# A gated feed-forward on TensorE: high weights against [high | low] in one 512-column matmul, in two of four layers

## The reference, cut to what matters

```python
def swiglu(h, w1, w3, w2):
    return (jax.nn.silu(h @ w1) * (h @ w3)) @ w2

# layers 2 and 3, behind their mixers
    h = rms_norm_2(x, norm_ffn_g_2[layer])
    x = x + swiglu(h, ffn_w1[layer], ffn_w3[layer], ffn_w2[layer])
```

## Time and profile before

| | us |
|---|---|
| median of 3 runs | 1327.35 (1326.54 to 1328.16) |
| span of the profiled execution, from its first to its last instruction | 1324.4 |
| TensorE busy in that span | 1296.3 (98%) |
| GpSimd busy | 1006.1 (76%) |
| ScalarE busy | 682.9 (52%) |
| VectorE busy | 637.0 (48%) |

### The profile page before, as it was taken

One profiled execution on the slowest core, in us unless ns is written; L12 is line 12 of the kernel. 1 busy time (PEld: TensorE's weight loads), 2 busy tenths in 40 slices (PEclk: granted clock), 3 DMA queues, 4 the chain that ended last, 5 costly groups with the idle time before them and its releaser, 6 DMA issues.

```text
span 1324.4 us, 27666 instructions
## 1 busy us (share of the span) xinstructions
PE 1296.3 (98%) x10976; PEld 1247.4 (94%) x10976; DVE 637.0 (48%) x1163; ACT 682.9 (52%) x944; POOL 1006.1 (76%) x793
## 2 busy tenths in 40 slices
PE   6999999999999999999999999999999999999999
PEld 6889999999988889999999978999999999999998
DVE  8994465555555748455565574211113455311112
ACT  7725643444666756443457565434446566543342
POOL 1327888888777659888887794988887766988885
PEclk9999999999999999999999999999999999999999
DMA  6305675545535235555454532555554433555530
GB/s 269 129 33 181 169 250 191 185 172 181 191 134 185 101 126 183 178 188 188 172 178 160 193 128 96 192 192 179 174 185 167 160 126 120 187 178 187 190 127 32
DMA packets 33879, 217.07 MB, mean 164 GB/s; under 512 B 3683, under 2 KB 7428, under 8 KB 8196
## 3 DMA queue, kind: packets, MB, share of 16 engines
q1 hardware_dynamic: 30096, 211.14, 45.1%
q10 hardware_dynamic: 3700, 4.75, 1.4%
HBM read 213.26 MB, written 2.62 MB: 163 GB/s over the span
## 4 chain that ended last, share of the span: by engine, by line
PE 85%; DVE 6%; ACT 6%; issue 2%; POOL 1%; DMA 0%; DVEq 0%; SPq 0%; ACTq 0%; POOLq 0%
PE up L1568 19%; PE up L1569 18%; PE up L1570 18%; PE acc L1568 7%; PE acc L1570 6%; PE acc L1569 6%; DVE opnd L972 2%; PE side L1795 2%; PE up L1703 1%; PE acc L1761 1%; ACT w_hi L503 1%; ACT opnd L641 1%; PE side L1576 1%; PE up L1834 1%; PE acc L1933 0%
## 5 line engine op out<-in xcount | busy, mean ns | idle before, releaser
L413 POOL TENSOR_TENSOR w_lo<-ring,w_hi 128x512 fp32r<-128x512 f32 x748 | 955.4, 1311 | 235.7 <-ACT w_hi L503 231.8
L1568 PE MATMUL up<-opnd,w_hi 128*128 128x256 f32 x2064 | 592.3, 287 | 3.7 <-DVE opnd L972 1.5
L1569 PE MATMUL up<-opnd,w_lo 128*128 128x256 f32 x2064 | 583.9, 283 | 0.0
L1570 PE MATMUL up<-opnd,w_hi 128*128 128x256 f32 x2064 | 583.8, 283 | 0.0
L503 ACT ACTIVATE w_hi<-ring 128x2048 fp32r<-128x2048 f32 x188 | 358.9, 1910 | 264.4 <-PE up L1570 202.7
L1568 PEld LDWEIGHTS up<-opnd,w_hi 128*128 128x128 f32 x2064 | 395.6, 192 | 16.1 <-issue 13.1
L1569 PEld LDWEIGHTS up<-opnd,w_lo 128*128 128x128 f32 x2064 | 395.8, 192 | 1.3 <-issue 1.0
L1570 PEld LDWEIGHTS up<-opnd,w_hi 128*128 128x128 f32 x2064 | 395.7, 192 | 0.0
L1568 PE MATMUL acc<-opnd,w_hi 128*128 128x256 f32 x784 | 223.0, 284 | 1.2 <-DVE x L1218 1.2
L1569 PE MATMUL acc<-opnd,w_lo 128*128 128x256 f32 x784 | 221.8, 283 | 0.0
L1570 PE MATMUL acc<-opnd,w_hi 128*128 128x256 f32 x784 | 221.8, 283 | 0.0
(11 more groups left out here) (296 smaller groups left out, 1421.3 us busy)
## 6 DMA issues: line engine op xcount, KB each, us to landing
ring<-in_stream SPq DMA_DIRECT2D x197, 1024.0 KB, 4.9
bias_rows<-mix ACTq DMA_DIRECT2D x1, 1536.0 KB
mix<-in_s_b SPq DMA_DIRECT2D x1, 1024.0 KB, 5.6
x<-in_x SPq DMA_DIRECT2D x1, 1024.0 KB, 7.7
mix<-in_s_c SPq DMA_DIRECT2D x1, 1024.0 KB, 11.7
mix<-bias_rows ACTq DMA_DIRECT2D x1, 1024.0 KB, 5.4
out_x<-x SPq DMA_DIRECT2D x8, 128.0 KB, 1.7
mix<-in_p ACTq DMA_DIRECT2D x2, 256.0 KB, 3.4
```

The source lines that it names most:

```text
L413: ins = nc.gpsimd.tensor_tensor(w_l[:, cols], ring[:, r, cols], w_h[:, cols].bitcast(f32), ALU.subtract)
L1568: MM(o, l_hi, r_hi, start=start, stop=False, skip_group_check=True)
L1569: MM(o, l_lo, r_hi, start=False, stop=False, skip_group_check=True)
L1570: return MM(o, l_hi, r_lo, start=False, stop=stop, skip_group_check=True)
```

## The change

In ffn2 and ffn3 alone (`WIDE`), the two products with the high weights become one matmul: the moving operand is [high | low], 512 columns, and writes 512 columns, high*high in the first half of a bank and high*low in the second. The product with the low weights stays at 256 columns and is added to the first half. A slot then has 32 matmuls, and its two halves take a bank each. Slots alternate between the two `up` banks and the two `side` banks. For this the operand is laid out as [partition, k, part, token], for all stages.

Behind the slot the halves are summed: ScalarE copies both second halves (the rest) to SBUF, VectorE adds them to the first halves, and multiplies by rstd in place, in PSUM. Silu reads there; the hidden product goes where the rest of the value was. So the banks of a tile are told free (`up_free`) at the end of the tile. ScalarE makes the copy ahead of the high part of slot k + 3. The first wide slot waits until every slot before it is told free. In the second slot PE makes the gate's half first, with `all_sums` behind its first group, and waits for rstd before it writes the value's half, since that bank held the sums.

```diff
+WIDE = (2, 3)
...
-        opnd = [sb("opnd0", [P, 2, KT, T], f32r)]
-        opnd.append(sb("opnd1", [P, 2, KT, T], f32r))
+        opnd = [sb("opnd0", [P, KT, 2, T], f32r)]
+        opnd.append(sb("opnd1", [P, KT, 2, T], f32r))
...
-        up = [ctx.enter_context(nc.psum_tensor(f"up{i}", [P, 2, T], f32)) for i in range(2)]
+        ups = ctx.enter_context(nc.psum_tensor("up", [P, 2, 2, T], f32))
+        up = [ups[:, i] for i in range(2)]
...
+        wide = [ups[:], side[:].rearrange("p m (a t) -> p m a t", a=2)]
...
                 def slot(k, i=None):
 
+                    j, part = (0, k) if k < 2 else ((k + 1) // 3, (k - 2) % 3)
+                    if l in WIDE and part != 2:
+                        act.wait_ge(sem("mm_done"), S + k + 1 if i is None else i * RING + (S + k + 1))
+                        c.up(A(f_c[:, 0:2], wide[part][:, :, 1], ACT.Copy), "rest_sb")
                     if i is None:
                         high_parts_to(S + k + 3)
...
+                    pair = wide[part]
+                    gate, val, h = (pair[:, 0, 0], pair[:, 1, 0], pair[:, 1, 1]) if l in WIDE else (gate_ps, val_ps, h_ps)
+                    if l in WIDE:
+                        c.wait("rest_sb")
+                        step(V.tensor_tensor(pair[:, :, 0], pair[:, :, 0], f_c[:, 0:2], ALU.add))
+                        r = rstd[:].unsqueeze(1).broadcast_to([P, 2, T])
...
+                            c.up_and_wait(V.tensor_tensor(pair[:, :, 0], pair[:, :, 0], r, ALU.mult), "g_ready")
...
-                    c.up_and_wait(V.tensor_tensor(hl, h_ps, hh.bitcast(f32), ALU.subtract), "h_ready")
+                    c.up_and_wait(V.tensor_tensor(hl, h, hh.bitcast(f32), ALU.subtract), "h_ready")
+                    if l in WIDE:
+                        c.tell("up_free")
...
+            def pair_products(o, l_hi, l_lo, r, start, stop):
+
+                MM(o, l_hi, r, start=start, stop=False, skip_group_check=True)
+                return MM(o[:, 0], l_lo, r[:, 0], start=False, stop=stop, skip_group_check=True)
...
+            def wide_slot(name, s, first, i=None, sums=False, fold=None, order=range(KT)):
+
+                slot_ready(s, i)
+                u = used[0]
+                used[0] += 1
+                pe.wait_ge(sem("up_free"), u if u == first else u - 1 if i is None else i * 4 + (u - 1))
+                o, w_h, w_l, both = wide[(u - first) % 2], weights_hi(s), weights_lo(s), opnd[SET[name]]
+
+                def part(k, m):
+                    w = slice((2 * k + m) * P, (2 * k + m + 1) * P)
+                    return pair_products(o[:, m], w_h[:, w], w_l[:, w], both[:, k], k == order[0], k == order[-1])
+
+                if sums:
+                    for j, k in enumerate(order):
+                        c.wait("hi_ready")
+                        c.wait("lo_ready")
+                        for m in range(2):
+                            ins = part(k, m)
+                        if j == KT // 2 - 1:
+                            square_sums(0)
+                else:
+                    for m in range(2):
+                        if fold is not None and m:
+                            pe.wait_ge(sem("rstd"), fold)
+                        for k in range(KT):
+                            ins = part(k, m)
+                            if fold is not None and m == 0 and k == 0:
+                                all_sums()
+                c.up(ins, "mm_done")
+                if sums:
+                    square_sums(1)
```

More of the change, by code:

```diff
@@ L659, in tile @@
                 def tile(parity, part):
+                    gate, h_out = (wide[part][:, 0, 0], wide[part][:, 1, 1]) if l in WIDE else (gate_ps, h_ps)
                     c.wait("g_ready")
-                    c.up(A(f_gg[:, 0], gate_ps, ACT.Gelu_apprx_tanh if l < 2 else ACT.Silu), "gated")
+                    c.up(A(f_gg[:, 0], gate, ACT.Gelu_apprx_tanh if l < 2 else ACT.Silu), "gated")
                     c.wait("h_raw")
-                    c.up(A(opnd[1][:, 0, 2 * parity + part], h_ps, ACT.Copy), "h_hi")
+                    c.up(A(opnd[1][:, 2 * parity + part, 0], h_out, ACT.Copy), "h_hi")
                 def slot(k, i=None):
+                    j, part = (0, k) if k < 2 else ((k + 1) // 3, (k - 2) % 3)
+                    if l in WIDE and part != 2:
+                        act.wait_ge(sem("mm_done"), S + k + 1 if i is None else i * RING + (S + k + 1))
+                        c.up(A(f_c[:, 0:2], wide[part][:, :, 1], ACT.Copy), "rest_sb")
                     if i is None:
@@ L697, in pe_operand @@
                 for k in range(2):
-                    c.up(A(opnd[1][:, 0, 6 + k], f_pe[:, k], ACT.Copy), "pe_hi")
+                    c.up(A(opnd[1][:, 6 + k, 0], f_pe[:, k], ACT.Copy), "pe_hi")
             def ple(l, end):
@@ L1176, in tile @@
                     dve.wait_ge(sem("mm_done"), s + k + 1 if i is None else i * 6 + (s + k + 1))
+                    pair = wide[part]
[4 more added lines that the diff above has]
+                        r = rstd[:].unsqueeze(1).broadcast_to([P, 2, T])
+                        if conv:
+                            step(V.tensor_tensor(f_u[:, 0:2, 2:258], pair[:, :, 0], r, ALU.mult))
+                        else:
+                            c.up_and_wait(V.tensor_tensor(pair[:, :, 0], pair[:, :, 0], r, ALU.mult), "g_ready")
+                    elif conv:
+                        over_rms(f_u[:, 0:2, 2:258], u)
+                    else:
+                        over_rms(side[:, :, 0:T], u)
+                        c.tell("g_ready")
                     if conv:
-                        over_rms(f_u[:, 0:2, 2:258], u)
-                        for t, o in ((0, gate_ps), (1, val_ps)):
+                        for t, o in ((0, gate), (1, val)):
                             base = COLS["conv"][0] + (l * 22 * 8)
@@ L1208, in ffn @@
                 with dve.Fori(0, 4) as i:
-                    c.enter(i, **(dict(dve_step=20, up_free=4, g_ready=4, gated=4, h_raw=4, h_hi=4, h_ready=4) if conv
-                                  else dict(up_free=4, g_ready=4, gated=4, h_raw=4, h_hi=4, h_ready=4)))
+                    steps = 4 * (5 * conv + (l in WIDE) * (1 + conv))
+                    c.enter(i, up_free=4, g_ready=4, gated=4, h_raw=4, h_hi=4, h_ready=4,
+                            **({"dve_step": steps} if steps else {}), **({"rest_sb": 4} if l in WIDE else {}))
                     for j in (3, 4):
@@ L1852, in ffn, with up_part @@
                 order = [m for g in groups for m in (2 * g, 2 * g + 1)]
[L1853 to L1857, removed]
+                first = BANK[f"ffn{l}"]
+                assert used[0] == first
+                def up_part(s, i=None):
+                    if l in WIDE:
+                        wide_slot(name, s, first, i)
+                    else:
+                        up_slot(name, s, i)
+                if l in WIDE:
+                    wide_slot(name, S, first, sums=True, order=order)
+                    wide_slot(name, S + 1, first, fold=(2, 5, 8, 10)[l])
+                else:
+                    up_slot(name, S, fresh=True, sums=True, order=order)
+                    up_slot(name, S + 1, fold=True)
+                up_part(S + 2)
+                up_part(S + 3)
                 def down(s, parity, first=False, i=None):
@@ L1863, in ffn @@
                 down(S + 4, 0, first=True)
-                up_slot(name, S + 5)
-                up_slot(name, S + 6)
+                up_part(S + 5)
+                up_part(S + 6)
                 down(S + 7, 1)
```

23 lines of the change are left out of this document (10 added, 13 removed).

## The result

The changed kernel takes 1332.59 us (median of 5 runs, 1332.29 to 1332.91), the kernel before 1327.1 on the same chip (5 runs, 1326.54 to 1328.16). The ratio is 1.0041, 95% interval [1.0029, 1.0054]: slower by 5.5 us, a small difference that the interval tells from none. The forecast was 1330.4, +3.1 us, with the range 1323 to 1336. The sign was right, the size not quite. Of all executions in this document one stands apart in time: in the experiment "First wait and third slot" one took 1781.3 us at a mean granted clock of 0.66; it counts in that kernel's median, which it moves by less than 0.1 us, and not in its ratio.

The account below looks back on a forecast made before the run. The prediction took TensorE, busy 98% of the span, to bound the kernel. Matmuls -5.3, first waits +5.1 and third slots +3.3 gave +3.1 us: 1330.4 us, range 1323 to 1336 (the forecast's own 1328 to 1333).

Parts of the forecast that it names:

- The matmuls: Up slots of ffn2 and ffn3: a group falls from 0.360 to 0.3525 us, 704 groups, 5.3 us saved.
- Rival A: Wide matmuls follow at 0.216 us, groups 0.336: 16.9 us saved, total -8.5 us, 1318.9; chance 0.14.
- B: Rival: a wide matmul costs exactly two narrow ones, 0.360 us a group, nothing saved: +8.4 us, 1335.8; chance 0.12.
- The first waits: First wide slot waits for up_free of all earlier slots: 3.7 us lost in ffn2, 1.4 in ffn3, together 5.1.
- so it ends at 826.8 instead of 823.1: 3.7 us lost: ffn2's first slot, begun at about 820.2, was to take 6.59 us, as undisturbed in ffn3.
- The third slots: Slot 2 waits for slot 0's late tile to free its banks: 1.7 us in ffn3, 3.3 in both feed-forwards.
- The loop: Added ScalarE and VectorE work lies beside PE: no PE idle in the loops, GpSimd's waits for w_hi still 0.7.
- From span to median: The runs' median lies 2.95 us above the profiled span, so a span of 1327.5 gives 1330.4.
- Rival C: The four waits cost about 1 us less each, +4.4 instead of +8.4: total -0.9 us, 1326.4; chance 0.10.

Follow-up runs that it names:

- First wait and third slot: Changed kernel with the first wide slot's up_free wait two counts lower and ScalarE taking the first tile ahead of slot 3's high weights: 1324.22 us, ratio 0.9979.
- first experiment: Changed kernel with the first wide slot of each wide feed-forward waiting for up_free two counts lower: 1325.55 us, ratio 0.9988 to the kernel before.
- second: Kernel before with only the stricter up_free wait at the first slot of ffn2 and ffn3 added: 1333.88 us, ratio 1.0052.
- third: Changed kernel with 22 small fp32 matmuls into a free bank ahead of ffn2's first wait: 1330.9 us, ratio 1.0030 to the kernel before.
- four-layer version: Changed kernel with loosened first wait, first tile early and slot 3's high weights on VectorE, widened in all four feed-forwards (ffn0 keeps the full wait): 1333.96 us, ratio 1.0056.
- kernel with 384 columns: Changed kernel with the wide matmul cut from 512 to 384 columns, part of a product left out: 1293.19 us, one run.

## Why the prediction was nearly right

- *The matmuls*: 0.3525 us a group was forecast, 0.3533 measured; 704 x 6.7 ns = 4.7 us against 5.3. Rival A (0.336) and B (0.360) are out: at 512 columns the distance is 236 ns, not 216, and the two ways of making the same sums differ by 6.7 ns a group. The formula behind the 216 is given in the Trainium skill ("TensorE: Matmul & The Clock Gate", section "Back-to-back issue gap") for an isolated matmul, which the prediction didn't say; for a stream of weight loads and matmuls the same section has about 131 ns at 512 columns. The 236 ns of this trace agree with neither. The short burst of the earlier trace rows was a good guide to both: 235 ns and 117.5 by it, 236 and 117 in the loop.
- *The first waits*: the start of both slots came out as worked out: 820.46 for about 820.2, and 1.43 us in ffn3 for 1.4. What failed is the step "so it ends at 826.8 instead of 823.1: 3.7 us lost". It took the slot to run at the upper clock behind a pause of five microseconds. The clock was at half for 6.83 us, and the slot took 2.7 us more than forecast. The two first waits together cost 7.8 us, not 5.1, which is outside this term's own bounds of 3 and 7: those allowed for half a microsecond to one only, and for no fall of the clock. That the total stayed in its range, and just inside the narrower 1328 to 1333, is to that extent luck: the range was wide enough to hold a cost that nobody had put into it. Taking the pause away restored the clock (first experiment), the pause alone brought the fall (second), and filling it with matmuls kept the clock but not the time of the wait (third).
- *The third slots*: 1.6 each for 1.7; the rest's copy took 0.58 for 0.62, VectorE's two operations were covered as said. The experiment in which ScalarE takes the tile first removed the wait.
- *The loop*: no wait of PE in it, as said. GpSimd waits for the high weights 19.5 us over 29 slots, 0.67 us each, as before:

```profile
POOL w_lo L418 <- ACT w_hi L508: 19.5, 29, 1.6
```

- *From span to median*: the 2.95 us between them are not all around the span. The execution after took 1332.91 us for a span of 1331.1, 1.8 around it; about half of the rest is that the execution of before was quick in its front (0.6 us quicker than the mean of the eleven other profiled executions). By the traces the forecast lacked 3.2 us (clock 2.7, groups 0.6, third slots -0.1), by the medians 1332.6 - 1330.4 = 2.2. The interval of the ratio is 3.8 to 7.2 us of difference and holds both 5.5 and the 6.3 of the account; the remaining 0.8 us isn't settled.
- *Rival C* (each wait 1 us shorter): out. Less the 0.35 us that the trace was late already, DVE's additions ended at 819.95, against 820.01 before, and all four waits came out as long as worked out, to 0.1 us.

## What to carry to other kernels

Two fp32r matmuls merged into a wider one cost nearly what their columns cost: here one instruction less in three saved 6.7 ns of 360. What decided the change was where its new waits stood, above all a wait for a count that no data needed; price a new pause of TensorE as its length plus, where it is as long as the 5.6 us here, a stretch at the lower clock behind it (at 2 to 4 us it went either way). And before widening, look which bank is still being read when the first wide slot starts: two counts less in that wait were worth 7.9 us, the whole matmul change 4.7.

## What the runs showed of the hardware that was not expected

- The granted clock fell to 0.50 with idle times of TensorE of 5.6 us, for 6.83 us each time, in wide and narrow matmuls alike (six traces); the price was 2.7 us. In the four-layer version it fell for 3.41 us with idle times of 2.2, 3.9 and 2.2 us (up to 1.4 us after their end), and did not fall with one of 2.7 us; nor did it with two of 2.2 us in the kernel with 384 columns (834.87 to 837.38 and 1128.27 to 1130.79), nor with those of 1.3 and 1.4 us. So the length of the idle time alone doesn't tell between 2 and 4 us; what does is open.
- fp32r matmuls: 236, 176 and 117 to 120 ns for 512, 384 and 256 columns; next to a wide one, 128 and 192 columns cost 104 and 108, nearly the same, with the two weight loads 108 ns apart in both.
- One VectorE operation with two tensors and a scalar, 128x768, took 0.95 to 0.96 us alone, and 1.08, 1.15, 1.51, 1.78 and 2.07 us where it met a GpSimd operation at work that went on for 0.2 us or more: it ended 0.81 to 0.83 us behind the end of that one.
